# Query times old state as four fp32r products: the state split into a high and a low part

## The reference, cut to what matters

```python
w_inter = jnp.exp(a - m_row)
s = jnp.einsum('bhik,bhjk->bhij', qc, kc) * w_intra
num = w_inter[..., None] * jnp.einsum('bhik,bhkv->bhiv', qc, C) + jnp.einsum('bhij,bhjv->bhiv', s, vc)
...
kw = kc * w_k[..., None]
C_new = decay[..., None, None] * C + jnp.einsum('bhjk,bhjv->bhkv', kw, vc)
```

## Time and profile before

| | |
|---|---|
| median of 3 runs | 2539.99 us |
| profiled execution, first to last instruction | 2538.4 us |
| mean granted TensorE clock | 0.995 of full speed |
| TensorE busy | 2512.6 us (99%) |
| VectorE busy | 1178.1 us (46%) |
| ScalarE busy | 857.3 us (34%) |
| GpSimd busy | 474.8 us (19%) |
| DMA, mean over the span | 152 GB/s |

### The profile page before, as it was taken

How to read it: one execution, slowest core, us unless ns; L and a number is a source line. 1 busy time by engine, 2 the same in 40 slices (tenths; PEclk the granted TensorE clock), 3 DMA queues, 4 the chain that set the end, 5 groups by cost and what they waited for, 6 DMA issues and landing times.

```text
span 2538.4 us, 43579 instructions
## 1 busy us (share of the span) xinstructions
PE 2512.6 (99%) x16623; PEld 2425.2 (96%) x16623; DVE 1178.1 (46%) x1375; ACT 857.3 (34%) x989; POOL 474.8 (19%) x536
## 2 busy tenths in 40 slices
PE   9999999999999999999999999999999999999998
PEld 8999999999999999999777779999999999999997
DVE  6644444444444454443555675544444444444443
ACT  4333333333333343333223343333333333333332
POOL 5430022012102232210010113321022003101321
PEclk9999999999999999999999999999999999999998
DMA  5554455454445444554466565554454444444452
GB/s 184 151 149 149 149 149 149 149 149 149 150 149 150 149 147 133 149 149 153 131 187 181 180 207 156 148 150 149 149 148 150 149 149 148 149 149 149 133 158 91
DMA packets 197124, 385.01 MB, mean 152 GB/s; under 512 B 12053, under 2 KB 12165, under 8 KB 196645
## 3 DMA queue, kind: packets, MB, share of 16 engines
q1 hardware_dynamic: 196780, 383.88, 49.9%
q0 software_dynamic: 272, 0.14, 0.0%
HBM read 361.78 MB, written 22.64 MB: 151 GB/s over the span
## 4 chain that ended last, share of the span: by engine, by line
PE 95%; DMA 3%; DVE 1%; ACT 0%; SPq 0%; issue 0%; ACTq 0%
PE G L1308 29%; PE G L1309 29%; PE G L1310 29%; PE X L1546 2%; PE X L1555 1%; DMA out_C_sample<-cst 1%; DMA out_C_prompt<-cst 1%; DMA cst<-in_state_mlstm_C 1%; PE X L1296 1%; PE X L1531 1%; DVE w_lo L907 0%; DMA gain<-in_norm_mix 0%; PE X L1508 0%; PE X L1415 0%; PE X L1467 0%; DVE cst L1241 0%
## 5 line engine op out<-in xcount | busy, mean ns | idle before, releaser
L907 DVE TENSOR_TENSOR w_lo<-w_raw,w_hi 128x1024 fp32r<-128x1024 f32 x648 | 826.4, 1277 | 1175.0 <-ACT w_hi L670 1174.1
L670 ACT ACTIVATE w_hi<-w_raw 128x1024 fp32r<-128x1024 f32 x640 | 677.7, 1059 | 1344.8 <-PE G L1310 1337.9
L1308 PE MATMUL G<-op_hi,w_hi 128*128 128x320 f32 x2816 | 871.9, 310 | 2.2 <-DVE w_lo L907 1.5
L1309 PE MATMUL G<-op_lo,w_hi 128*128 128x320 f32 x2816 | 870.1, 309 | 0.0
L1310 PE MATMUL G<-op_hi,w_lo 128*128 128x320 f32 x2816 | 870.1, 309 | 0.0
L1308 PE MATMUL G<-a_hi,w_hi 128*128 128x320 f32 x2368 | 732.6, 309 | 0.0
L1310 PE MATMUL G<-a_hi,w_lo 128*128 128x320 f32 x2368 | 731.7, 309 | 0.0
L1309 PE MATMUL G<-a_lo,w_hi 128*128 128x320 f32 x2368 | 731.7, 309 | 0.0
L1308 PEld LDWEIGHTS G<-op_hi,w_hi 128*128 128x128 f32 x2816 | 528.5, 188 | 6.7 <-issue 2.5
L1309 PEld LDWEIGHTS G<-op_lo,w_hi 128*128 128x128 f32 x2816 | 528.6, 188 | 1.5
L1310 PEld LDWEIGHTS G<-op_hi,w_lo 128*128 128x128 f32 x2816 | 528.5, 188 | 0.0
(11 more groups left out here) (243 smaller groups left out, 860.2 us busy)
## 6 DMA issues: line engine op xcount, KB each, us to landing
w_raw<-in_ffn_w_up SPq DMA_DIRECT2D x256, 512.0 KB, 3.7
w_raw<-in_ffn_w_down SPq DMA_DIRECT2D x256, 512.0 KB, 3.8
w_raw<-in_mlstm_w_in SPq DMA_DIRECT2D x96, 512.0 KB, 3.8
cst<-in_state_mlstm_C SPq DMA_DIRECT2D x32, 512.0 KB, 4.0
out_C_sample<-cst SPq DMA_DIRECT2D x32, 512.0 KB, 6.2
w_raw<-in_mlstm_w_out SPq DMA_DIRECT2D x32, 512.0 KB, 4.5
w_raw<-in_pool_w SPq DMA_DIRECT2D x8, 512.0 KB, 10.5
xrow<-in_x_prompt SPq DMA_DIRECT2D x2, 1024.0 KB, 6.0
```

The costliest lines, as they stand in the source:

```text
L670: act.activation(w_hi[:, c % RING], w_raw[:, c % RING], ACT.Copy).then_inc(w_hi_ok, 1)
L907: v.tensor_tensor(w_lo[:, slot], w_raw[:, slot], w_hi[:, slot].bitcast(F32), ALU.subtract).then_inc(w_lo_ok, 1)
L1308: pe.matmul(G[:, m, 0:T], w_hi[:, slot, t, w], hi[:, k, :], start=first and t == 0, stop=False)
L1309: pe.matmul(G[:, m, 0:T], w_hi[:, slot, t, w], lo[:, k, :], start=False, stop=False)
```

## The change

The old state is split as the weights are: ScalarE writes `c_hi` (fp32r), GpSimd `c_lo` = C - `c_hi`, one buffer each. The queries get a high and a low part, too (`q2`, VectorE). GpSimd keeps one operand `qz` of 128 columns, 64 high and 64 low, with zeros but for the 8 columns of the current sequence in each half (`query`). The product of a state is four fp32r matmuls (2 row blocks, `c_hi` and `c_lo`) into 128 rows of `X[2]`; rows 0 to 63 collect the high queries' part and rows 64 to 127 the low queries'. `samples_turned` adds the halves while it turns them: instead of a transpose, a product with the mask `fold` (two stacked identities). SyncE's order is changed: a state is loaded two ahead instead of three, behind the store of state c, into the slot of state c-1, and the next slab's weights come behind it. Some small tiles are moved or narrowed to make room (`sel` is replaced by a broadcast column of `ident`, `rden` has one buffer, `dec` is split off `EW`).

```diff
-        sel = head_rows("sel", [HEADS, P])
+        fold = sb("fold", [P, NS])
...
+            c_hi = sb("c_hi", [P, 2, DV], F32R, r)
+            c_lo = sb("c_lo", [P, 2, DV], F32R, r)
...
-            qwm = sb("qwm", [P, 2, NSEQ * (NS + TS)], F32, r)
+            q2 = sb("q2", [P, 2, 2, NS], F32R, r)
+            qz = sb("qz", [P, 2, 2, NS], F32R, r)
...
@@ SyncE
-            for q in range(HEADS + 1):
+            for c in range(CH):
+                load(S_O, c, w_qkvo[c][:, :, 8 * NC:9 * NC])
+            for h in range(HEADS):
                 for c in range(CH):
-                    if q < HEADS:
-                        load(S_O + q, c, w_qkvo[c][:, :, (8 + q) * NC:(9 + q) * NC])
+                    if c == 0:
+                        if h:
+                            state_load(h, 1)
+                        state_store(h, "prompt")
+                    state_store(h, c)
+                    if c + 2 < NSEQ:
+                        state_load(h, c + 2)
+                    elif c == NSEQ - 1 and h + 1 < HEADS:
+                        state_load(h + 1, 0)
+                    if h + 1 < HEADS:
+                        load(S_O + h + 1, c, w_qkvo[c][:, :, (9 + h) * NC:(10 + h) * NC])
                     else:
                         load(S_OUT, c, w_out[c][:, :, 0:NC])
-                    if q == 0:
-                        continue
-                    if c == 0:
-                        state_store(q - 1, "prompt")
-                        state_load(q - 1, 2)
-                    state_store(q - 1, c)
-                    if c + 3 < NSEQ:
-                        state_load(q - 1, c + 3)
-                    elif c > 5 and q < HEADS:
-                        state_load(q, c - 6)
@@ GpSimd
+            def query(h, b):
+
+                pool.wait_ge(q2_ok, 2 * (h + 1))
+                n, old = state_no(h, b), slice((b - 1) % NSEQ * TS, ((b - 1) % NSEQ + 1) * TS)
+                if n:
+                    pool.wait_ge(qc_done, n)
+                at = slice(b * TS, (b + 1) * TS)
+                pool.memset(qz[:, :, :, old].bitcast(F32), 0.0).then_inc(qz_ok, 1)
+                pool.tensor_copy(qz[:, :, :, at], q2[:, :, :, at]).then_inc(qz_ok, 1)
+
+            def state_lo(h, b):
+
+                pool.wait_ge(c_hi_ok, state_no(h, b) + 1)
+                pool.tensor_tensor(c_lo[:, :, :], cst[:, c_slot(b)], c_hi[:, :, :].bitcast(F32),
+                                   ALU.subtract).then_inc(c_lo_ok, 1)
...
             for h in range(HEADS):
-                if h:
-                    head_squares(h - 1)
-                if h + 1 < HEADS:
-                    weigh_keys(h + 1)
+                for b in range(NSEQ):
+                    query(h, b)
+                    state_lo(h, b)
+                    if h and b == 0:
+                        head_squares(h - 1)
+                    if h + 1 < HEADS and b == 3:
+                        weigh_keys(h + 1)
@@ ScalarE
+            def state_hi(h, b):
+
+                n = state_no(h, b)
+                act.wait_ge(c_in[c_slot(b)], 16 * c_loads(h, b))
+                if n:
+                    act.wait_ge(qc_done, n)
+                act.activation(c_hi[:, :, :], cst[:, c_slot(b)], ACT.Copy).then_inc(c_hi_ok, 1)
...
                 for c in range(CH):
                     n = LEAD + c
+                    state_hi(h, c)
                     split(S_O + h, n) if n < CH else split(S_O + h + 1, n - CH)
...
-                act.activation(hs[0:NS, :], X[2][0:NS, :], ACT.Copy).then_inc(hs_kept, 1)
+                act.activation(hs[:, :], X[2][:, :], ACT.Copy).then_inc(hs_kept, 1)
@@ VectorE
                 if h:
-                    v.wait_ge(x2_filled, h)
-                for t in range(2):
-                    ins = v.tensor_copy(qwm[:, t, :].rearrange("p (b r) -> p b r", r=NS + TS)[:, :, 0:TS],
-                                        qw[:, t, :].rearrange("p (b t) -> p b t", t=TS))
-                ins.then_inc(qwm_ok, 1)
+                    v.wait_ge(qc_done, NSEQ * h)
+                v.tensor_copy(q2[:, :, 0, :], qw[:, :, :]).then_inc(q2_ok, 1)
+                v.wait_ge(q2_ok, 2 * h + 1)
+                v.tensor_tensor(q2[:, :, 1, :], qw[:, :, :], q2[:, :, 0, :].bitcast(F32), ALU.subtract).then_inc(q2_ok, 1)
...
+                    v.wait_ge(c_lo_ok, state_no(h, c) + 1)
                     v.wait_ge(filled, FILL["upd", h, c])
@@ TensorE
                 for n in range(4):
-                    ins = turn(X[2][:, n * NS:(n + 1) * NS], hs[0:NS, n * P:(n + 1) * P], NS)
+                    ins = pe.matmul(X[2][:, n * NS:(n + 1) * NS], hs[:, n * P:(n + 1) * P], fold[:, :], start=True, stop=True,
+                                    skip_group_check=True)
                 ins.then_inc(x2_turned, 1)
...
-                        pe.matmul(X[2][0:NS, :], ST[0:NS, 384:448], kvs[0:NS, p, 0:DV], start=True, stop=False)
-                        pe.wait_ge(qwm_ok, h + 1)
+                        pe.matmul(X[2][:, :], ST[:, 384:512], kvs[:, p, 0:DV], start=True, stop=False)
...
-                    pe.wait_ge(c_in[c_slot(c)], 16 * c_loads(h, c))
+                    pe.wait_ge(c_lo_ok, state_no(h, c) + 1)
+                    pe.wait_ge(qz_ok, 2 * (state_no(h, c) + 1))
                     for t in range(2):
-                        ins = pe.matmul(X[2][0:NS, :], qwm[:, t, c * NS:(c + 1) * NS], cst[:, c_slot(c), t, :],
-                                        start=False, stop=c == CH - 1 and t == 1)
-                    if c == CH - 1:
-                        ins.then_inc(x2_filled, 1)
+                        for n, c2 in enumerate((c_hi, c_lo)):
+                            ins = pe.matmul(X[2][:, :], qz[:, t, :, :].rearrange("p a i -> p (a i)"), c2[:, t, :],
+                                            start=False, stop=c == CH - 1 and t == 1 and n == 1)
+                    ins.then_inc(qc_done, 1)
```

More of the change, by code:

```diff
@@ L211, in build @@
             u = sb("u", [P, TT, D], F32, r)
+            vrow = sb("vrow", [P, P], F32, r)
         with ExitStack() as r:
@@ L316, in build @@
         x3_read = sem("x3_read")
-        x2_filled = sem("x2_filled")
+        qc_done = sem("qc_done")
+        c_hi_ok = sem("c_hi_ok")
+        c_lo_ok = sem("c_lo_ok")
+        q2_ok = sem("q2_ok")
+        qz_ok = sem("qz_ok")
         att_s = sem("att_s")
@@ L357, in tok, with state_no @@
             return slice(t * P, t * P + ROWS[t])
+        def state_no(h, b):
+            return NSEQ * h + b
         def head_block(h):
@@ L537, in _ @@
                 select(seqmask[at:at + NS, 2, 1:], [[TS, NSEQ]], -1, base=TS - 1)
-            link(pool.memset(sel[:, :, :], 0.0))
-            select(sel[:, :, :], [[-1, HEADS], [0, P]], 1, op=ALU.not_equal, fill=1.0)
+            link(pool.memset(fold[:, :], 0.0))
+            for at in (0, NS):
+                select(fold[:, :], [[-1, NS]], 1, base=-at, op=ALU.not_equal, fill=1.0)
             with nc.allow_non_contiguous_dma("a few values"):
@@ L622, in _ @@
             link(pool.memset(cols[:, :, :], 0.0))
-            link(pool.memset(qwm[:, :, :], 0.0))
+            link(pool.memset(ST[:, 384:512], 0.0))
+            link(pool.memset(qz[:, :, :, :].bitcast(F32), 0.0))
             pool.memset(nrow[0:1, :], 0.0).then_inc(rows_ok, 1)
@@ L1185, in _ @@
                 p = h % 2
-                rd = rden[p]
                 v.wait_ge(x3_filled, X3_USES[f"den{h}"])
                 v.wait_ge(drained_a, ACT_FILL["rows", h, 0])
-                link(v.scalar_tensor_tensor(out=rd[:, :], in0=X[3][:, 0:T], scalar=-1.0, in1=EW[:, p, 0:T],
+                link(v.scalar_tensor_tensor(out=rd[:, :], in0=X[3][:, 0:T], scalar=-1.0, in1=EW[:, 0:T],
                                             op0=ALU.mult, op1=ALU.max))
@@ L1210, in _ @@
                     samples_out(h - 1)
+                    v.wait_ge(att_s, h)
+                link(v.tensor_copy(rds[:, :], rd[:, TP:T]))
                 v.wait_ge(x3_filled, X3_USES[f"n{h}"])
@@ L1240, in _ @@
                         st = cst[:, c_slot(c), t, :]
-                        ins = v.scalar_tensor_tensor(out=st, in0=st, scalar=EW[:, p, T + NS + 1 + c:T + NS + 2 + c],
+                        ins = v.scalar_tensor_tensor(out=st, in0=st, scalar=dec[:, p, 1 + c:2 + c],
                                                      in1=X[t][:, :], op0=ALU.mult, op1=ALU.add)
@@ L1459, in prep @@
                     bank_free(("rows", h, 0))
-                    pe.matmul(X[0][:, 0:T], sel[:, h, :], gates[:, R_NEGM:R_E], start=True, stop=True)
-                    ins = pe.matmul(X[1][:, 0:BC], sel[:, h, :], gates[:, R_E:R_WK], start=True, stop=True)
+                    one_head = ident[GP:GP + HEADS, GP + h:GP + h + 1].broadcast_to([HEADS, P])
+                    pe.matmul(X[0][:, 0:T], one_head, gates[:, R_NEGM:R_E], start=True, stop=True)
+                    ins = pe.matmul(X[1][:, 0:BC], one_head, gates[:, R_E:R_WK], start=True, stop=True)
                 else:
@@ L1498, in _ @@
```

(2 more changed lines are left out.)

20 lines of the change are left out of this document (10 added, 10 removed).

## The result

The changed kernel takes 2560.24 us as the median of 4 runs (2553.9 to 2565.19) where the kernel before, in turn with it, takes 2540.26. Two of the four lie near 2555 and two near 2565, so the median stands between them. The ratio is 1.0073, interval 1.0052 to 1.0094: a small loss, but clear of the noise. The forecast was 2529, in 2517 to 2542, so both its sign and its range were wrong. The profiled execution has a span of 2552.2 us (its time is 2553.9), 13.8 over the span before.

The account below looks back on a forecast made before the run. TensorE was taken to bound the kernel. Savings of 10.1 us from the periods plus 4.2 from the heads' first states, minus 3.2 for the turns, gave 11.1 less: 2529 us, range 2517 to 2542.

Parts of the forecast that it names:

- What bounds it: TensorE is on the path for 95% of the span; only shortening its work or a stall moves the time.
- (a): On TensorE, four fp32r products replace two fp32 per state, 0.94 for 1.86 us; a state's floor falls by 1.05.
- (b): SyncE's loads wait only for the store of state c-1; most of its 141.6 us behind its own stores goes.
- (c): The four turns of sample rows become fp32 products on TensorE, adding 0.8 us per head, 3.2 in all.
- (d): Between state load and query product: `c_hi` 1.05, `c_lo` 2.3, handovers 0.2, together 3.55 us; the single buffer is hidden.
- (e): Loop from update n to n+2, with a 4.8 us load: 12.2 us; wrong if head 3 is at 38 or over 50.
- (f): At state 5 of heads 1 and 2, engines crowd, its store is 4.7 us late; each head gains only 0.3.
- B: Rival: a new wait in the load loop takes the whole gain, slower than before, 2545; chance 0.16, milder form 0.22.
- A: Rival: crowding at state 5 doesn't add up; heads 1 and 2 end near 46.6 us, 2516 in all; chance 0.15.
- C: Rival: four fp32r products with 128 stationary columns are no quicker than the two in fp32; chance 0.02.

Follow-up runs that it names:

- e4: Changed kernel with useless fp32 products on TensorE ahead of its waits for `c_lo` at states 1 and 7 of heads 1 to 3: 2544.12 us, ratio 1.0012.
- e8: Changed kernel with SyncE's old order of loads and stores: 2579.72 us, ratio 1.0161.
- e7: Kernel before, fp32 products kept, with SyncE's new order alone: 2533.94 us, ratio 0.9985.
- e1: Changed kernel with the load of the next head's state 1 moved ahead of the last weight chunk in SyncE's queue: 2541.03 us, ratio 1.0001.
- e5: Changed kernel with state 1's load ahead of the last weight chunk, gating behind the update of state 5, and low part on VectorE: 2518.64 us, ratio 0.9922.

## Why the prediction was wrong, step by step

The periods were forecast at 200.1 us in all and took 225.2. State by state, over the four heads, the 25 us too much are 9.4 at state 1, 5.6 at state 2, 2.7 and 0.2 at 3 and 4, 1.3 at 5, 2.9 at 6 and 3.0 at 7. So the start of the heads was missed above all, and the slow records are in each of these numbers.

**What bounds it; (a) the removed products: right.** Four fp32r products take 0.93 to 0.94 us, and 1.12 behind fp32 records. In head 0 the short periods (states 1 and 6) are 6.0 and 5.4, as forecast. Those of states 3 to 5 are 8.1, 7.2 and 7.9, some 0.25 to 0.75 above their floors of 7.3, 6.85 and 7.65 (a floor is what TensorE's own records take without a wait); they are so in all kernels with the split, but for state 3 in e4 and e8, which took 9.6. A part is that the query product stands behind fp32 pieces there and takes 1.04 us and more up to the update, where 0.94 was counted. The rest I have not traced.

**(b) SyncE's order: right in direction.** The 141.6 us are gone, and e7 shows 5 us for it. (Of the 4.3 us that head 3 was said to wait before, TensorE's rows show 3.5.) That this order also put the load of state 1 behind a weight chunk was not weighed: the sum counted 1.05 won at the first state of each head and a state 1 on its floor. From rows 8, where GpSimd's squares of the previous head hold VectorE's splits, the 2.9 us split could have been read; head 3's end stood for the end of every head. This is the first step that failed: 9.5, 9.6 and 8.3 us for state 1 in heads 1 to 3 where 6.1 and 5.7 were counted, 9.5 us in all; state 2 follows with 9.3 in head 1 where 6.5 was counted. e1 undoes it for 13.8, clock included.

**(c) the turns: right in size** (1.0 per head where 1.18 was counted, and 1.35 behind the last head, among slow records).

**(d) the chain: right in size.** `c_hi` 1057 ns (1.05 taken), `c_lo` 2391 ns (2.3 taken): the page's groups of ScalarE and GpSimd.

```profile
L859 ACT ACTIVATE c_hi<-cst 128x1024 fp32r<-128x1024 f32 x32 | 33.8, 1057 | 101.5 <-DMA cst<-in_state_mlstm_C 83.2
L673 POOL TENSOR_TENSOR c_lo<-cst,c_hi 128x1024 fp32r<-128x1024 f32 x32 | 76.5, 2391 | 72.0 <-ACT c_hi L859 72.0
```

**(e) the loop: the load was right as a median (4.6 where 4.8 was taken), the loop too short.** The two late loads of head 1, of states 1 and 7, took 5.7 and 5.4. The loop ended at the query product. But a late load also holds the iteration of ScalarE and VectorE: weight split, key, and the copy for which the update product waits. At state 1 the load lands at 1300.77, and the query product starts 3.6 behind that, the update product 5.6. The two engines' programs run in order, and what stands behind the waiting instruction was not counted as delayed. Head 3 is 53.8, beyond the 50 that was named as the mark against this step. Heads without that snag are nearer: head 0 is 2.5 above its forecast.

**(f) the snag at state 5: right in place and mechanism, and nearly in size.** The lock of the earlier trace rows holds (1.22 becomes 2.35 to 2.9), ScalarE's hold is as read, and it is the load of state 7 that suffers. Period 5 was counted as 9.2 and took 9.1; states 5 to 7 of heads 1 and 2 were counted as 26.2 and took 27.9 and 28.3. What was not foreseen is that small operations are held by a whole `c_lo` too (`qn`, 2.61 us), and that TensorE runs at half rate behind the 4.65 us. Forecasting it, I still called the heads even with before, because the floor of the first five states paid for it.

**The missing term: the clock.** No step and no rival had a price for what a stall does to the records behind it. The profile before runs at 1.00 in this stretch and could not show it there. At full rate the forecast's error would be smaller by at least the 10.7 us of e4, that is more than a third of the 26 to 31 us by which 2529 was missed. The Trainium skill (TensorE: Matmul & The Clock Gate, "HAM oscillation") describes a kernel that loses its fast clock in each wait for data, and slows down by more than the waits; by it the loss would be above the sum of the waits, and the traces agree: the periods lose 28 x 1.05 = 29.4 us of floor and gain 26.8 us of waits (32.9 against 6.1), which alone would be 2.6 less, and they are 14.6 longer.

The size of the missing term can be estimated from the same rows. Undisturbed periods of e5 and e7 (6.0 against 7.15, 5.4 against 6.5, 8.0 against 8.4, 7.2 against 7.9, 7.9 against 8.7) give 27 us of floor for the 28 periods and not 29.4. Floor and waits then cancel, and some 15 us are left, as large as the bound of 14.7 from the granted clock; the slow stretches in TensorE's timeline, eight of 2.6 to 5.3 us and 26 in all, give 13 at half rate. So the waits took the whole gain, and the slow records behind them made about all of the loss.

**The rivals.** B named the right side, a wait at the new chain that takes the whole gain, and both its parts occur (loads of 5.4 to 5.7 and VectorE's split kept from the port). It had 2545 as its end and 0.16. The range left out more than it said: B beyond it and A just outside it are 0.31, not two in ten. What B lacked is the start of the head and the clock: it priced only waits. A is refuted for the change as made, though e5 shows its heads 1 and 2 at 49.4 and 51.0 when VectorE does the low part: the gain was there to be had. C is refuted. The sum went wrong by taking all side paths at their undisturbed length, with one exception at state 5.

## What to carry to other kernels

When work is taken off the bound engine and a new operand is put in its place, count the whole iteration behind the new wait on every engine that runs in order, and each transfer queued behind a slot that such an iteration frees. Give each expected stall of TensorE a second price, the half-rate records that may follow it; a few useless products in the stall measure that price. Before an elementwise product with two SBUF inputs goes to GpSimd, look what VectorE has to do beside it. In this kernel the slower engine held up the quicker, and moving the product onto the busier engine turned 1.0059 into 0.9967.

## What the runs showed of the hardware

Stalls of 2.15 + 0.85 us, with a product between them, and of 4.65 us were followed by records at the lower clock (0.43 us apart for 512 columns instead of 0.23); with the first filled with products to 1.01 + 0.86 it did not fall (e4). But the length of a wait did not decide it: of three waits of 2.57 to 2.58 us in e5 one left the clock at 1.00 and two did not, and at state 2 of head 0 in e4, where nothing is filled, waits of 0.74 + 0.86 us were followed by slow records (granted clock 0.79 in 1250 to 1258). These runs give no rule for when it falls. I had expected a stall to cost its own length. And VectorE's instruction is held even where it is tiny: a copy of 64 columns takes 1.93 us beside GpSimd's subtraction, 0.20 without it. That is a surprise, because the earlier trace rows show it between large operations with two inputs each, and this copy has one. Not all is held: a product of 256 columns with one of its inputs in PSUM (L1216), begun beside the same subtraction, took 0.42 us, and 0.43 in e5.
